# A hybrid encoder block on one NeuronCore: the causal edge of the attention scores written into PSUM by VectorE instead of added by mask products on TensorE

## What is computed

```python
def diff_attention(q, k, v, lam):
    qb = q.reshape(b, nb, Q_BLOCK, H_A, 2, DH_A).transpose(1, 0, 2, 3, 4, 5)   # Q_BLOCK = 128
    key_chunk = jnp.arange(s) // CHUNK                                        # CHUNK = 64
    def one_block(args):
        q_blk, i = args
        sc = jnp.einsum('bqhcd,bkhcd->bhcqk', q_blk, k).astype(jnp.float32) * scale
        q_chunk = (i * Q_BLOCK + jnp.arange(Q_BLOCK)) // CHUNK
        allowed = key_chunk[None, :] <= q_chunk[:, None]
        sc = jnp.where(allowed, sc, jnp.finfo(jnp.float32).min)
        p = jax.nn.softmax(sc, axis=-1)
        p_diff = p[:, :, 0] - lam * p[:, :, 1]
        return jnp.einsum('bhqk,bkhe->bqhe', p_diff.astype(v.dtype), v)
```

## Time and profile before

| | |
|---|---|
| median of 3 runs | 3129.53 us (3128.91 to 3129.88) |
| span of the profiled execution | 3129.4 us |
| own device time of the profiled execution | not given beside the span; the median is 0.1 us above the span |
| attention, from its first score product to its last output copy | 889.9 to 1283.4 us of the span |
| busy over the span | PE 94%, DVE 50%, ACT 31%, POOL 20% |
| mean granted TensorE clock | 0.979 of full speed |

### The profile page before, as it was taken

One profiled execution on the slowest core, in us unless ns is written; L12 is line 12 of the kernel. 1 busy time (PEld: TensorE's weight loads), 2 busy tenths in 40 slices (PEclk: granted clock), 3 DMA queues, 4 the chain that ended last, 5 costly groups with the idle time before them and its releaser, 6 DMA issues. The chain is left out here.

```text
span 3129.4 us, 66008 instructions
## 1 busy us (share of the span) xinstructions
PE 2931.8 (94%) x25434; PEld 1889.1 (60%) x25435; DVE 1556.1 (50%) x3592; ACT 957.6 (31%) x2271; POOL 637.5 (20%) x780
## 2 busy tenths in 40 slices
PE   8999999999969999799999989997699999999999
PEld 6778877777746666688888855554233333333333
DVE  4676767677778889433333357775111111111111
ACT  3343334333447777322222223332000000000000
POOL 0000000000035555200000000001233333333333
PEclk9999999999989999899999999998799999999999
DMA  7121111112131000411111113335498878776763
GB/s 241 61 70 62 62 62 63 61 58 73 61 104 41 28 15 1 142 37 45 45 45 37 37 55 108 108 95 202 126 328 295 301 273 320 281 272 251 254 238 120
DMA packets 190197, 397.46 MB, mean 127 GB/s; under 512 B 16155, under 2 KB 76443, under 8 KB 188913
## 3 DMA queue, kind: packets, MB, share of 16 engines
q1 hardware_dynamic: 169440, 343.47, 31.7%
q0 software_dynamic: 20512, 50.54, 4.7%
HBM read 327.25 MB, written 80.32 MB: 130 GB/s over the span
## 5 line engine op out<-in xcount | busy, mean ns | idle before, releaser
L325 PE MATMUL pj_big<-pj_xnT,pj_w_in 128*128 128x256 f32 x2816 | 634.8, 381 | 4.6 <-ACT pj_ubuf L397 3.0
L325 PEld LDWEIGHTS pj_big<-pj_xnT,pj_w_in 128*128 128x128 f32 x2816 | 537.4, 191 | 85.7 <-ACT pj_ubuf L397 6.9
L1810 PE MATMUL ex_pgu<-keep_res,ex_xT 128*64 128x512 f32 x2560 | 568.9, 597 | 0.0
L1810 PEld LDWEIGHTS ex_pgu<-keep_res,ex_xT 128*64 128x64 f32 x2560 | 177.1, 137 | 334.9 <-issue 334.9
L1918 DVE TENSOR_TENSOR ex_hh<-ex_sg,ex_pgu 128x256 f32<-128x256 f32 x80 | 33.7, 421 | 584.0 <-ACT ex_sg L1883 584.0
L1828 PE MATMUL ex_py<-keep_res,ex_hT 128*64 128x512 f32 x1280 | 288.3, 592 | 1.0 <-DVE ex_yb L1926 1.0
L758 POOL TENSOR_SCALAR at_tt<-at_e,at_cf 128x512 f32<-128x512 f32 (+3 forms) x160 | 219.3, 1374 | 185.7 <-DVE at_pd L802 163.5
L1329 PE MATMUL mg_po<-keep_res,mg_mix 128*128 128x512 f32 x512 | 234.1, 614 | 7.0 <-DVE mg_mix L1632 7.0
L737 ACT ACTIVATE at_e<-at_sc,at_nmx 128x512 f32<-128x512 f32 (+3 forms) x320 | 196.9, 623 | 68.9 <-DVE at_nmx L780 66.6
L295 POOL TENSOR_TENSOR pj_m<-pj_qn,pj_cosin 128x256 f32<-128x256 f32 x64 | 46.6, 728 | 827.6 <-DVE pj_qn L524 601.4
L1883 ACT ACTIVATE ex_sg<-ex_pgu 128x256 f32<-128x256 f32 x80 | 30.7, 384 | 582.5 <-PE ex_pgu L1810 582.5
(11 more groups left out here) (293 smaller groups left out, 4720.1 us busy)
## 6 DMA issues: line engine op xcount, KB each, us to landing
keep_res<-in_w_exp_gate SPq DMA_DIRECT2D x32, 2048.0 KB, 8.6
keep_res<-in_w_exp_up SPq DMA_DIRECT2D x32, 2048.0 KB, 15.5
keep_res<-in_w_exp_down SPq DMA_DIRECT2D x32, 2048.0 KB, 8.6
chunks_s<-pj_st SPq DMA_DIRECT2D x32, 642.0 KB, 4.0
rw_raw<-chunks_s SPq DMA_DIRECT2D x32, 642.0 KB, 3.9
pj_xt<-in_x SPq DMA_DIRECT2D x20, 512.0 KB, 3.8
qk_s<-pj_qo SPq DMA_DIRECT2D x64, 128.0 KB, 1.9
mg_xin<-in_x SPq DMA_DIRECT2D x8, 1024.0 KB, 7.1
```

The lines of the kernel that those rows point to most:

```text
L325: ins = pe.matmul(out, lhs, rhs, start=(k == 0), stop=(k == KC - 1))
L1810: ins = pe.matmul(pgu[j * BT:(j + 1) * BT, :, :], lhs, wgu[x][:, k, :, j * HE:(j + 1) * HE], start=(k == 0), stop=(k == KC - 1))
```

## The change

The constant `mask` and its transfer go, and with them the two mask products of an edge unit. In their place VectorE writes -1e30 into the corner of the finished scores, a rectangle of 64 partitions by 2 x 64 elements in PSUM, and waits on a semaphore of its own for that write before it takes the maximum.

```diff
@@ attend: tiles and semaphores
-        mask = m.sb("mask", [P, 2, P])
+        s_edge = m.sem("edge_done")
@@ SyncE
-            for dst, src in ((lams[:, :, :], io["lams"]), (mask[:, :, :], io["c_mask"]), (ident[:, :], io["c_ident"])):
+            for dst, src in ((lams[:, :, :], io["lams"]), (ident[:, :], io["c_ident"])):
                 sp.dma_start(dst, src).then_inc(s_const, 16)
@@ TensorE
-            pe.wait_ge(s_const, 48)
+            pe.wait_ge(s_const, 32)
-                    diag = s == i // 4
                     for c, rows in enumerate(halves):
                         ins = pe.matmul(sc[u % 2][:, c, 0:w], qT[h % 2][rows, i * P:(i + 1) * P],
-                                        kT[h % 2][rows, s * SEG:s * SEG + w], start=True, stop=not diag)
-                    if diag:
-                        for c, rows in enumerate(halves):
-                            ins = pe.matmul(sc[u % 2][:, c, w - C:w], mask[rows, 0, :], mask[rows, 1, C:],
-                                            start=False, stop=True)
+                                        kT[h % 2][rows, s * SEG:s * SEG + w], start=True, stop=True)
                     ins.then_inc(s_sc, 1)
@@ VectorE
                     dve.wait_ge(s_sc, u + 1)
+                    if s == t % NT // 4:
+                        dve.memset(sc[u % 2][0:C, :, w - C:w], NEG).then_inc(s_edge, 1)
+                        dve.wait_ge(s_edge, t + 1)
                     dve.tensor_reduce(nmx[:, t % RE, :, s], sc[u % 2][:, :, 0:w], AX, ALU.max, negate=True)\
                         .then_inc(s_mx, 1)
```

More of the change, by code:

```diff
@@ L50 @@
 E_HALF = float(np.exp(-0.5))
+NEG = -1e30
 LAMBDA_INIT = 0.8 - 0.6 * float(np.exp(-0.3 * 0))
@@ L762, in _ @@
         def _(dve):
-            dve.wait_ge(s_const, 48)
+            dve.wait_ge(s_const, 32)
             pairs = lams[:, :, :].rearrange("p (a b) n -> p a b n", b=2)
@@ L1080, in _ @@
             half(NCH - 1, 1, has_pre=False)
-NEG = -1e30
 class Early:
@@ L2006, in constants @@
     ones2 = np.kron(np.eye(2), np.ones((64, 64))).astype(np.float32)
-    mask = np.zeros((P, 2, P), np.float32)
-    mask[::64, 0, 0:C] = -1e30
-    mask[::64, 1, C:] = 1.0
     row, col = np.arange(P)[:, None] % C, np.arange(C)[None, :]
@@ L2027, in constants @@
             "c_blank": np.tile(np.array([S, 0], np.float32), TABLE).reshape(P, -1),
-             "c_mask": mask,
             "c_eye": one(row == col), "c_mgb": mgb, "c_mgk": mgk, "c_mgl": mgl}
```

## The result

The changed kernel takes 3134.84 us (median of 19 runs), the kernel before, run beside it, 3129.88 (19 runs). The ratio is 1.0015 with a 95% interval from 1.0009 to 1.0021: by that ratio slower by 4.7 us, between 2.8 and 6.6 (the two medians alone are 5.0 apart). Forecast were +2.1 us and no measurable change; the interval leaves out both. The profiled execution has a span of 3133.0 us where the one before had 3129.4.

What follows compares the result with a forecast made beforehand. Each attention head was taken as bound partly by VectorE, partly by both nearly full, partly by TensorE. +0.65 us a head, +2.6 for four, less 0.5 at the start, gave +2.1: 3131.6 us, range 3126.5 to 3138.5.

Steps and rivals of the forecast that it cites:

- tiles 8 to 11: Part of each attention head: VectorE's four writes use up its 1.00 us of gaps and it becomes the bound; 0.
- M: TensorE's gain per edge unit of attention without the mask products, from scores to transposes: 0.17 us.
- E: VectorE's price per edge unit for the corner write and its wait: 0.25 us, range 0.20 to 0.32.
- Tiles 4 and 5: Part of each attention head: VectorE's writes hide in a 0.77 us gap, TensorE wins one edge; -0.17 us.
- Tiles 12 to 14: Part of each attention head: VectorE's gaps hold all the writes, TensorE's gain is kept; 3 x -0.17 = -0.51 us.
- Tiles 6 and 7: Part of each attention head: VectorE is full, so both writes are paid; 2 x 0.25 = +0.50 us.
- Tiles 15 and 0 to 3: Attention head's last and first tiles: +0.08 us at 15, 0 at 0 (gap covers the write), +0.75 at 1 to 3.
- The start: Start of attention: one DMA less, the mask's, ahead of the loads the first scores wait for; -0.5 us.
- The first rival: VectorE's write into PSUM costs a whole short PSUM operation, 0.42 us; +9.9 us, 3139.4 us; chance 0.22.
- The second: VectorE's write costs only its elements, as an unlinked step, 0.135 us; -2.5 us, 3127.0 us; chance 0.15.
- The third's first form: TensorE bounds attention everywhere, so 10.9 us are won, 11.4 with the DMA; 3118.1 us; chance 0.07.
- Its second form: Attention's mask products are worth their busy 0.35 us per edge unit; -3.5 us, 3126.0 us; chance 0.06.

## Why the prediction was right and where it was not

The range held the time, and the sign of the sum and its mechanism were right: the bound changes within a head, and the change is paid on one side and won on the other. But the size was taken too small, +2.1 us, where the measured interval begins at 2.8, and it would have been further off without an error the other way, in tiles 8 to 11. Its steps:

- M = 0.17 us, from the distance of starts and not from the busy 0.35 us: right, in every tile where it is won.
- E = 0.25 us, from the rows of memsets below and the copy above: mis-sized. It is 0.31, the upper end. The start distance from write to maximum was 0.20 as worked out at the low end. What I left out is the overlap in front of the write: rows 5 show that an unlinked step starts before its neighbour's end, and the write takes that away in front of itself as well.
- Tiles 4 and 5, -0.17: measured -0.17. The gap of 0.77 us took 0.62 + 0.17 and was spent to the last hundredths.
- Tiles 12 to 14, -0.51: measured -0.51.
- Tiles 8 to 11, 0: measured -0.08, and the mechanism is not the forecast one. With E = 0.31 its rule, VectorE as the bound, gives 4 x 0.31 - 1.00 = +0.24, and the measured kernel without products and without the write shows that two of the three products are won here (-0.34). What stands together is the two halves added, +0.25 - 0.34 = -0.09. This is one of the signs of being wrong that the prediction named: TensorE's gain does reach the end in these tiles, in part.
- Tiles 6 and 7, +0.50: measured +0.62, two times E.
- Tiles 15 and 0 to 3, +0.08 and +0.75: measured 1.01 together, +0.08 of it at tile 15; with E = 0.31 the list gives 0.14 + 0.93 = 1.07.
- A head then has +0.87 where +0.65 was forecast, four heads 3.5 us instead of 2.6. The forecast's own list with E = 0.31 would give +1.27 a head, 5.1 us in all, so the two errors cancel in part, and that the time came this near is partly luck. The distances measured are +3.9, +3.2 and +3.8.
- The start, -0.5: borne out, -0.56 between the middle values from the first issue to the first scores. It does not show in a single pair of profiles, in which the first maximum moves by 2 us without any change.

Together that is 3.5 - 0.56 = +2.9 us by the heads, and +2.6 from attention's first issue to its last copy, for a forecast of +2.1. The measured interval begins at 2.8. The rest, up to 4.7 us, isn't settled: outside attention two profiles of the kernel before differ by 6.7 us, and the falls of the clock behind the longer waits, 0.9 us on the mean by the estimate above, would fit into it but are in none of the three profiles of the changed kernel.

The first rival, a dear write, has the right direction and the wrong mechanism: it put the price on the completion in PSUM, and PSUM is 0.06 us of it. The second, by the rule of the Trainium skill that a semaphore behind a VectorE operation costs nothing (VectorE: DVE Perf Modes, The DRAIN you can't avoid), does not hold for these short operations: the same write costs 0.07 us without its wait and 0.25 with it. By its number, 0.135 us a write, the rival is wrong too. The third's first form would have seen TensorE's 10.9 us; the kernel without the write shows 4.7. Its second form, products worth 0.35 us, falls with the 0.17 of every step.

## What to carry to other kernels

In a stage where two engines take turns as the bound, an exchange of work between them is neither good nor bad as a whole: read each part of a loop for who has idle time there, and move the work only where the receiver has some. The price of a small operation is the distance from its predecessor's start to its successor's, less what that distance was without it; its row's length was half of that here. To judge a change of some microseconds, compare the starts of the same instruction in two profiles of a stage: in two profiles of the kernel before they agreed to 0.01 us, once shifted by the same 2.02, where whole executions differed by several. A time that is counted from the start of the kernel carries the scatter of all that ran before; counted from its own stage's first instruction, a gain of half a microsecond could be told.

## What the runs showed of the hardware

- A VectorE write of 64 x 128 elements with a row of 165 ns costs 0.07 us where nobody waits for it, 0.25 with a wait behind it, 0.31 when it goes to PSUM, in a stretch where VectorE is full.
- A pair of mask products, busy for 0.35 us, takes 0.17 us from start to start.
- The first maximum moved between 886.6 and 891.4 us over fourteen profiles whose stage ahead was the same. From the first issue to the first scores it was 8.60 to 9.13 us without one small transfer ahead of the loads and 9.28 to 10.32 with it.
- TensorE's clock fell to 0.50, its level of 1.2 GHz, for more than 3 us after a wait of 1.51 us in 3 of 18 passages, and never in 18 after one of 1.34; after 1.82 and 2.35 us it fell in one of three each. That the longer wait is the cause is not shown.
